# Moving the first filter's preparation into the projection, summing its squares on TensorE, and mixing signal and filter stages in the opening of a long convolution

## The reference

```python
def implicit_filters(...):
    ...
    hdn = jnp.sin(f32(freq[0]) * (feats @ f32(w1) + f32(b1)))
    hdn = jnp.sin(f32(freq[1]) * (hdn @ f32(w2) + f32(b2)))
    filt = (hdn @ f32(w3)).reshape(L, HYENA_ORDER, D_HYENA)
    ...
    filt = filt * jnp.exp(-offset[:, None, None] * rates)
    return filt * lax.rsqrt(jnp.sum(filt * filt, axis=0, keepdims=True) + RMS_EPS)

def hyena_mixer(u_hy, zh, rows, conv_w, conv_b, filt, fbias):
    ...
    z = x1 * fft_long_conv(v, filt[:, 0], fb[0])
    y = x2 * fft_long_conv(z, filt[:, 1], fb[1])
    return y * jax.nn.silu(zh)
```

## Time and profile before

| | before |
|---|---|
| median of 3 runs | 1657.27 us (1656.33 to 1658.02) |
| the profiled execution: its own time | 1656.43 us |
| its span, first to last instruction | 1654.7 us |
| PE busy | 1577.1 us (95%) |
| DVE busy | 711.5 us (43%) |
| ACT busy | 672.9 us (41%) |
| POOL busy | 307.3 us (19%) |
| mean granted TensorE clock | 0.984 of full |

### The profile page before, as it was taken

How to read it: one execution, slowest core, us unless ns; L and a number is a source line. 1 busy time by engine, 2 the same in 40 slices (tenths; PEclk the granted TensorE clock), 3 DMA queues, 4 the chain that set the end, 5 groups by cost and what they waited for, 6 DMA issues and landing times. The chain is left out here.

```text
span 1654.7 us, 23549 instructions
## 1 busy us (share of the span) xinstructions
PE 1577.1 (95%) x8886; PEld 1357.0 (82%) x8886; DVE 711.5 (43%) x1123; ACT 672.9 (41%) x1371; POOL 307.3 (19%) x297
## 2 busy tenths in 40 slices
PE   8799999999999999999999599999999787999997
PEld 3688888888888888888887599989898776888886
DVE  1754420333333333010100686777675566555553
ACT  2885212333222222131211455555555375545551
POOL 1552000000000000000000031311212125666661
PEclk9899999999999999999999799999999999999999
DMA  9231621222222122121111563647445475566651
GB/s 362 83 116 59 217 70 49 80 76 76 70 76 76 70 76 95 51 98 49 45 51 49 226 154 91 186 103 203 91 116 151 170 216 160 180 208 201 195 179 52
DMA packets 128192, 201.72 MB, mean 122 GB/s; under 512 B 12556, under 2 KB 75714, under 8 KB 121191
## 3 DMA queue, kind: packets, MB, share of 16 engines
q1 hardware_dynamic: 128102, 200.52, 38.3%
HBM read 122.45 MB, written 52.86 MB: 106 GB/s over the span
## 5 line engine op out<-in xcount | busy, mean ns | idle before, releaser
L454 PE MATMUL bank<-h_hi,w_hi 128*128 128x512 f32 (+1 forms) x840 | 324.8, 387 | 0.0
L456 PE MATMUL bank<-h_hi,w_lo 128*128 128x512 f32 (+1 forms) x840 | 322.9, 384 | 0.0
L455 PE MATMUL bank<-h_lo,w_hi 128*128 128x512 f32 (+1 forms) x840 | 322.9, 384 | 0.0
L455 PEld LDWEIGHTS bank<-h_lo,w_hi 128*128 128x128 f32 x840 | 158.3, 188 | 31.2 <-issue 0.2
L456 PEld LDWEIGHTS bank<-h_hi,w_lo 128*128 128x128 f32 x840 | 158.2, 188 | 31.3
L454 PEld LDWEIGHTS bank<-h_hi,w_hi 128*128 128x128 f32 x840 | 158.3, 188 | 30.8 <-issue 0.2
L822 DVE SCALAR_TENSOR_TENSOR work<-work,coef 128x504 f32<-128x504 f32 (+1 forms) x84 | 62.3, 742 | 239.8 <-ACT work L610 239.7
L454 PE MATMUL bank<-w_hi,h_hi 128*128 128x512 f32 (+1 forms) x448 | 164.5, 367 | 0.0
L455 PE MATMUL bank<-w_lo,h_hi 128*128 128x512 f32 (+1 forms) x448 | 164.1, 366 | 0.0
L456 PE MATMUL bank<-w_hi,h_lo 128*128 128x512 f32 (+1 forms) x448 | 164.1, 366 | 0.0
L600 ACT ACTIVATE work<-bank 128x512 f32<-128x512 f32 (+1 forms) x72 | 40.4, 562 | 299.2 <-PE bank L456 299.2
(11 more groups left out here) (228 smaller groups left out, 2841.2 us busy)
## 6 DMA issues: line engine op xcount, KB each, us to landing
H<-spectrum SPq DMA_DIRECT2D x192, 128.0 KB, 2.4
stage<-in_w_in SPq DMA_DIRECT2D x18, 1024.0 KB, 5.6
s_hy<-work SPq DMA_DIRECT2D x48, 256.0 KB, 2.2
xin<-s_hy SPq DMA_DIRECT2D x8, 1024.0 KB, 5.1
kq<-s_k SPq DMA_DIRECT2D x32, 256.0 KB, 4.4
v<-s_v SPq DMA_DIRECT2D x32, 256.0 KB, 5.1
mb<-s_rows SPq DMA_DIRECT2D x32, 256.0 KB, 5.7
late<-in_x SPq DMA_DIRECT2D x16, 512.0 KB, 4.9
```

What stands on the lines that cost most here:

```text
L454: pe.matmul(out, lhs[0], rhs[0], start=(k == 0), stop=False)
L455: pe.matmul(out, lhs[0], rhs[1], start=False, stop=False)
L456: return pe.matmul(out, lhs[1], rhs[0], start=False, stop=(k == KD - 1))
```

## The change

`hidden`'s split, the first load of `w3`, window and bias, and the first signal `xin` move into the projection, into memory that the projection's own weights leave free (class `Opening`; `stage` and `w_hi` change places with the tiles behind them). Weights and window are loaded behind the store of tile 1 of the last 16, the signal behind that of tile 8, and the splits stand in ACT's and DVE's order after tile 9. `ident` is loaded once and kept through all blocks. In the opening, the squares of order 0 are taken in four parts and summed by 16 accumulating PE matmuls with ones in place of DVE's sum and one matmul. ACT evaluates one root on a single column first. `x_outer` of the first signal stands between norm and `f_outer`; `x_rows` and the second `turn` stand behind `f_inner`. The `w3` of group 1 is loaded and split in the opening as well, and the gate operands of group 0 are loaded behind the spread of the first spectrum. In `mixer` some small tiles lie elsewhere, the identity's load is gone, and a first write waits for the last `y` store.

```diff
+    def load_third(self, sp, d, g):
+        sp.dma_start(self.w3[:, :], d["fw3"][g]).then_inc(self.group_in, 16)
+        sp.dma_start(self.window[:, :, :], d["window"][g]).then_inc(self.group_in, 16)
...
@@ project, SP
                 store(bank_free, Z0 + m + 1, s["zh"][m // 4, :, m % 4 * TILE:(m % 4 + 1) * TILE],
                       (Z0 + m) % 4, TILE)
+                if m == 1:
+                    sp.wait_ge(w_lo_ready, 19)
+                    sp.wait_ge(gate_out, 16)
+                    opening.load_third(sp, d, 0)
+                    opening.load_bias(sp, d, 0)
+                if m == 8:
...
+                    sp.wait_ge(tile_ready, Z0 + B_TILES // 2)
+                    opening.load_x(sp, s, 0)
@@ project, ACT
                 if m == 7:
                     sines(1)
+                if m == 9:
+                    act.wait_ge(hid_ready, 4)
+                    act.wait_ge(w_lo_ready, 19)
+                    for e in range(2):
+                        high = slice(e * HALF_P, (e + 1) * HALF_P)
+                        act.copy(opening.layer[high, e, :], hidden[high, :]).then_inc(opening.layer_hi, 1)
+                    act.wait_ge(opening.group_in, 32)
+                    act.copy(opening.w3_hi[:, :], opening.w3[:, :]).then_inc(opening.w3_high, 1)
@@ hyena, SP
-            load_group(0)
-            sp.dma_start(ident[:, :], d["ident"]).then_inc(start_in, 16)
-            load_x(0)
             sp.dma_start(outer[:, :], d["outer"].rearrange("p a k -> p (a k)")).then_inc(start_in, 16)
...
+            sp.wait_ge(w3_low, 1)
+            for t in (W_TILES - 2, W_TILES - 1):
+                wait_taken(sp, 0, ("P", "in_time", t))
+            opening.load_third(sp, d, 1)
             wait_filled(sp, 0, ("P", "turn", F_TILES - 1))
-            load_x(GROUPS)
-            load_gates(0)
+            opening.load_x(sp, s, GROUPS)
...
             spread_spectrum(0, "P")
+            load_gates(0)
@@ hyena, PE
-            norm(0, "P", 0, 0)
-            pe.wait_ge(f_ready, 1)
+            dst = bank[wait_bank(0, ("P", "norm", 0))][:, 0:P]
+            for n in range(N2):
+                if n % 4 == 0:
+                    pe.wait_ge(square_part, n // 4 + 1)
+                mm = pe.matmul(dst, ones[:, :], in_Bf[:, n, :], start=(n == 0), stop=(n == N2 - 1))
+            mm.then_inc(summed, 1)
+            pe.wait_ge(start_in, 16)
+            outer_signal(0, 0)
+            pe.wait_ge(f_ready, 1)
...
+            signal_rows(0, 0)
+            turn_next(0, 0)
@@ hyena, ACT
-            square(0, "P", 0, Bf)
+            act.activation(total[:, 0:1], guard[:, 0:1], ACT.Sqrt)
+            for i in range(4):
+                for t in (2 * i, 2 * i + 1):
+                    wait_taken(act, 0, ("P", "in_time", t))
+                cut = slice(4 * i, 4 * i + 4)
+                act.activation(in_Bf[:, cut], f[:, 0, cut], ACT.Square).then_inc(square_part, 1)
             take_turned(0, "P", nat)
-            square(0, "P", 1, B)
             root(0, "P", 0)
+            square(0, "P", 1, in_A2f)
+            take_outer(0, 0, "x_outer", B, 2)
             take_outer(0, "P", "f_outer", Bf, 1)
...
+            take_signal_rows(0, 0)
+            high_w3(0, 2)
+            take_turned(0, 0, x1)
@@ hyena, DVE
             take_turned(0, "P", nat)
-            sum_squares(0, 0, Bf)
             invert(0, "P", 0)
+            take_outer(0, 0, "x_outer", B, (1,))
             scale(0, 0, 0)
-            sum_squares(0, 1, B)
+            take_outer(0, 0, "x_outer", B, (3, 5, 7))
+            sum_squares(0, 1, in_A2f)
             invert(0, "P", 1)
             scale(0, 1, 1)
...
+            take_signal_rows(0, 0)
+            take_turned(0, 0, x1)
+            low_w3(0, 2)
```

More of the change, by code:

```diff
@@ L1072, in mixer @@
         kT, qT = kq[:, 0:2], kq[:, 2:4]
[L1073 to L1076, removed]
         h = kw[:, 0, 0]
@@ L1762, in unit_tiles, with opening_tiles @@
     return tiles
+def unit_tiles(o, ahead):
+    return unit_head(o, ahead or o == 0) + unit_body(o, ahead)
+def opening_tiles():
+    tiles = in_time_tiles("P") + signal_tiles("P", "turn") + [("P", "norm", 0)] + signal_tiles(0, "x_outer")
+    tiles += filter_outer_tiles("P") + [("P", "norm", 1)] + filter_rows_tiles("P") + inner_pairs("P", None)
+    tiles += signal_tiles(0, "x_rows") + signal_tiles(0, "turn")
+    return tiles + unit_body(0, True) + unit_tiles(1, True)
 def taker(tile):
@@ L1779 @@
 TAKEN = {e: sum(taker(tile) == e for tile in GROUP) for e in ("act", "dve")}
-FIRST = {e: sum(taker(tile) == e for tile in PROLOGUE) for e in ("act", "dve")}
+FIRST = {e: sum(taker(tile) == e for tile in OPENING) - TAKEN[e] for e in ("act", "dve")}
+FILLED_FIRST = len(OPENING) - len(GROUP)
 def placed(tiles, start, earlier):
@@ L2094, in unit @@
                     to_rows(g, (o, "x_rows", t), B, t)
+            pe.wait_ge(layer_lo, 2)
+            pe.wait_ge(w3_low, 1)
+            in_time(0, "P")
+            pe.wait_ge(x_in, 16)
+            turn_x(0, "P")
+            pe.wait_ge(const_set, 2)
+            dst = bank[wait_bank(0, ("P", "norm", 0))][:, 0:P]
[7 more added lines that the diff above has]
+            pe.wait_ge(f_ready, 1)
+            for t in range(S_TILES):
+                outer_tile(0, ("P", "f_outer", t), f[:, 0], t)
+            norm(0, "P", 1, 1)
+            filter_rows(0, "P")
+            pe.wait_ge(filter_in, 16)
+            for t in range(Q_TILES):
+                inner_tile(0, "P", "f_inner", "f_rows", A2f, t)
+            signal_rows(0, 0)
+            turn_next(0, 0)
+            pe.wait_ge(const_in, 32)
+            def unit(g, o, ahead):
+                more = ahead or o == 0
+                if not (isinstance(g, int) and g == 0 and o == 0):
+                    outer_signal(g, o)
+                    if more:
+                        turn_next(g, o)
+                    signal_rows(g, o)
                 if more:
@@ L2181, in take_turned, with take_signal_rows @@
                     take(g, (u, "turn", t), dst[:, 4 * t:4 * t + 4])
+            def take_signal_rows(g, o):
+                for t in range(0, Q_TILES, 2):
+                    take(g, (o, "x_rows", t), A2[:, 4 * t:4 * t + 4])
             def take_filter_rows(g, u):
@@ L2257, in take_turned, with take_signal_rows @@
                     take(g, (u, "turn", t), dst[:, 4 * t:4 * t + 4])
+            def take_signal_rows(g, o):
+                for t in range(1, Q_TILES, 2):
+                    take(g, (o, "x_rows", t), A2[:, 4 * t:4 * t + 4])
             def low_w3(g, loads):
@@ L2326, in unit @@
                 more = ahead or o == 0
-                take_outer(g, o, "x_outer", B)
-                if more:
-                    take_turned(g, o, nat if o else x1)
-                for t in range(1, Q_TILES, 2):
-                    take(g, (o, "x_rows", t), A2[:, 4 * t:4 * t + 4])
+                if not (isinstance(g, int) and g == 0 and o == 0):
+                    take_outer(g, o, "x_outer", B)
+                    if more:
+                        take_turned(g, o, nat if o else x1)
+                    take_signal_rows(g, o)
                 for t in range(Q_TILES):
```

319 lines of the change are left out of this document (157 added, 162 removed).

## The result

The changed kernel takes 1638.99 us, median of 4 runs (1637.02 to 1640.36), against 1657.38 us of the kernel before, median of 4 runs beside it (1656.33 to 1658.02). The ratio is 0.9891, with a 95% interval of 0.9875 to 0.9907. That is 18.4 us less, with an interval of 15.4 to 20.7. I had forecast 1642.8 with a range from 1639.5: the direction is right, and the gain is 3.9 us larger than the 14.5 forecast, half a microsecond outside the range.

What follows compares the result with a forecast made beforehand. PE, 95% busy, bounds the kernel, so time is won where it waits or runs at half clock. 6.1 + 6.3 + 1.6 - 0.2 + 0.7 = 14.5 us gives a median of 1642.8, range 1640 less half a us to 1648.

Steps and rivals of the forecast that it cites:

- The preparation ahead of the barrier: Seam between projection and long convolutions: splits and loads moved earlier cut PE's idle 9.91 us to 3.8, gaining 6.1 us.
- 3.5 to 4.2 said: Sign at the seam: PE's first in_time matmul comes 3.5 to 4.2 us behind its last projection matmul.
- branch and first fetch: Start behind the barrier: some tenths more, so PE's first matmul at 911.9 where 911.6 was the earliest.
- The fourth rival: Projection's last tiles stall as ACT waits for w3 and window; slower, 1661 us or more; chance 0.02.
- `in_time`, `turn`, norm, `x_outer`, `f_outer`, norm of order 1: Opening stages: norm and x_outer order gain 6.3 us, f_outer at full clock 1.6, norm of order 1 costs 0.2.
- The third rival: Opening: the new order does not help, DVE's chain stays in series with PE; 1650.5 us, chance 0.05.
- Behind that: After the first x_inner: the 0.75 us wait for group 1's w3 goes, gaining 0.7 us.
- from some 3.5 us later on and throughout: Sign: granted clock full from some 3.5 us after PE's first in_time matmul onward.
- Queues: SP's transfers of the first spectrum: margin shrinks to 0.9 us, no cost; 0.4 us at a 3.7 us landing.
- the second rival: First spectrum's spread lands late, shifting products and in_time by 0.5 to 2 us; about 1644.3 us, chance 0.08.
- the end of the sum: Whole kernel: 14.5 us taken off the profiled 1656.43 gives 1641.9; shifted by 0.84 to the median, 1642.8.
- Mixer: nothing: Third block: a missing 64 KB load and a wait for a store issued before the barrier change nothing.

Runs made afterwards that it cites:

- late_prep: Changed kernel with the splits of hidden and w3 and the three loads put back behind the barrier: 1645.78 us, ratio 0.9925.
- no_mix: Changed kernel with the first signal's x_outer, turn and x_rows in the old order behind f_inner, norm matmuls kept: 1644.29 us, ratio 0.9921.
- dve_sum: Changed kernel with the squares of order 0 again summed on DVE and one matmul: 1644.14 us, ratio 0.9914, one outlier run left out.
- old_places: Changed kernel with the third block's (mixer's) tiles back at the old addresses: 1640.84 us, ratio 0.9913.
- before_again: The kernel before, profiled once more without any edit: 1657.64 us, ratio 1.0006.
- before_new_places: The kernel before with only the mixer's og, zg, gate and small tiles moved to the changed kernel's order: 1655.91 us, ratio 1.0008.
- raw_up_64: The kernel before with a 64-byte gap ahead of the mixer's raw weights, so y_lo lies 64 bytes higher: 1655.64 us, ratio 1.0004.

## Why the prediction was off

The mechanism held in the opening; the sum made of it was too small, and it took one execution for the kernel. By the prediction's own steps, on the two profiled executions:

- **The preparation ahead of the barrier**, 6.1 forecast: the idle time fell from 9.91 to 3.50, 6.4 us. PE begins 3.50 us behind its last matmul (3.5 to 4.2 said). `late_prep` gives 6.4 back. I had added 0.3 for branch and first fetch; it isn't there. The fourth rival, stalled projection tiles, did not occur.
- **`in_time`, `turn`, norm, `x_outer`, `f_outer`, norm of order 1**: from the first `in_time` to the first `x_inner` 43.1 us became 34.9, 8.2 us where 6.3 + 1.6 - 0.2 = 7.7 were forecast. `in_time` took 5.4 us (911.87 to 917.27) in place of 5.5, the norm 3.6 where 3.7 were forecast, and `f_outer` waited for nothing. One detail was luck: `in_time` was to begin at 1.2 GHz, and it began at full clock, which fell 0.9 us later. The slow stretch lasted 3.4 us instead of 3.5 and lay wholly within `in_time`, so the cost came out the same. The third rival (the order does not help) is excluded by `no_mix` and `dve_sum`, which lose 7.1 and 4.5 us of the opening.
- **Behind that**, 0.7 forecast for the wait for `w3` of group 1: from the first `x_inner` to group 0's `in_time` 14.40 us became 13.41, 1.0 us.
- **The middle and the third block**, nothing forecast. The middle got 2.8 us longer (342.46 to 345.26), 2.6 of it in the slow stretch at the end of the long convolutions; the third block got 3.6 shorter (336.8 to 333.2). The clock was to be full "from some 3.5 us later on and throughout". In the opening it was full from 4.3 us after PE's start on; for the end of the long convolutions no term was there.
- **Queues**: nothing forecast, nothing seen; the second rival, a late `H`, did not occur.
- Sum: 6.4 + 8.2 + 1.0 = 15.6 us in the opening, for 14.5. **The terms of the sum were 1.1 us too small**: 0.3 for the preparation, 0.5 for the stages up to `x_inner`, 0.3 behind them.
- The chances do not quite add up: the outcomes that the prediction itself puts well below the old time have 0.96 together, and it gives "faster" 0.94.

**The step that failed** is the end of the sum: "The profiled execution takes 1656.43, so 1641.9; it lies 0.84 below the median of 1657.27, so the median forecast is 1642.8", with its terms 1.1 us too small. By it one execution's opening stood for the kernel's. With three more profiles of kernels that have the same opening, the old way to group 0's `in_time` takes 67.40, 68.21, 68.91 and 68.12 us, a mean of 68.16, the first being the shortest. The changed one takes 51.77, 51.76, 51.78, 51.76 and, in `old_places`, 50.28, a mean of 51.47. The mean gain of the opening is 16.7 us and not 15.6. What varied in the old opening is in two of the three cases the clock (`before_again`, `before_new_places`); in `raw_up_64` it is 0.6 us of idle time, in which ACT waits longer for the load ahead of the `w3` copy (4.09 us for 3.49). With the opening's mean gain in place of 14.5 the forecast would have been 1657.4 - 16.7 = 1640.7 us, and with the 1.2 us that the middle loses on average (table below) 1641.9.

The same four and five profiles give for the whole program, in us:

| stretch | before | changed | difference |
|---|---|---|---|
| up to the end of the projection | 907.97 | 907.75 | -0.2 |
| opening | 68.16 | 51.47 | -16.7 |
| middle | 343.50 | 344.71 | +1.2 |
| third block | 335.05 | 335.15 | +0.1 |
| span | 1654.7 | 1639.1 | -15.6 |

**The rest, 2 to 3 us of the 18.4, is not explained, and perhaps not there.** Three pairs of medians give gains of 18.4, 18.5 and 15.9 us; the third's interval is 13.9 to 18.2, and 16.7 lies in the intervals of all three. All 15 runs of the changed kernel have a mean of 1639.4 and the 32 of the kernel before beside them 1656.4: a gain of 17.1, with 1.8 as two standard errors, which agrees with the traces' 15.6. "Mixer: nothing" seemed refuted by the first pair of traces (336.8 to 333.2 us), and by matmuls of 390 for 396 ns, which over 256 of each kind would make up to 2.5 us (1, 6 and 3 ns of the three kinds). Over all profiles it is not: at full clock the third block takes 323.5 to 325.6 in four profiles of old kernels and 323.0 to 328.5 in ten of changed ones, mean 325.0 and 325.3. So what the matmuls show is not seen in the length of the block, whose own scatter is as large. Why they are shorter stays open; the addresses of `og`, `zg`, the small tiles and `gate`, and the offset of `y_lo`, are excluded, the other places were not tried.

The range was too narrow below for the same reason: a single execution of the changed kernel lies up to 7 us from the median beside it (1633.95 to 1642.99 around 1639.09, and 1646.05 for 1639.47). In the profiles of the changed kernel most of this is the third block (332.5 to 339.5 us), in part by its slow stretches: over all profiles it has 15 to 30 us at 1.2 GHz. I estimate the uncertainty of a median of four at 1 to 2 us from the scatter of these runs; 1640 less half a microsecond took no account of it.

## What to carry to other kernels

When a change closes gaps in TensorE's work, count behind each gap also the stage that then runs at 1.2 GHz: here `no_mix` cost 4.2 us of waiting and 2.9 of slow matmuls. Profile the kernel before more than once ahead of a sum to a few tenths of a per cent, since one execution's slow stretches can lie a microsecond or more from the usual. Then read the stages behind the change as well: here the end of the long convolutions, where PE's work had not changed, took 2.6 us more in the first pair of traces. And look at what a barrier waits for: a store that nothing behind the barrier reads soon, and whose source nothing overwrites before it is waited for, need not hold it (1.8 us of waiting here).

## What the runs showed of the hardware

The clock's fall is not tied to the gap that brings it. In the changed kernel PE stood still for 3.50 us at full clock and the clock fell 0.9 us after it had begun to work (0.6 to 1.0 in the four profiles with this opening); in `old_places`, with the same gap, it did not fall at all; in the kernel before it fell at 911.3 in one profile and at 912.0 in another, both times while PE stood still. This is what the Trainium skill says in "TensorE: Matmul & The Clock Gate", section "Part 1: The HAM clock gate (the 'warmup' mystery)": the monitor runs on its own time, and does not start anew with the kernel. The runs agree, and give the price here: 1.5 us between a fall and none. A slow stretch lasted 3.4 us in the changed kernel's opening. One long gap is not needed either: at the end of the long convolutions the changed kernel's clock fell at 1288.2, behind waits of 1 us at most.

ACT's table load for the root took 1.28 us (911.68 to 912.96), ahead of the first square, while ACT had nothing else to do. In the kernel before it took the same, and cost nothing there either, since it lay within the wait for DVE's sum (926.87 to 930.51):

```profile
929.63 1.28 ACT L2177 ACT_TABLE_LOAD   x1
```

So no run shows that asking for the root early gained anything.
